# Forward block with a product-key expert layer: which token block is chosen first, and the order of its gathers and scatters

## The chip, the cores and the metric

The kernel runs on one core of one Trainium2 chip. The metric is the device time in microseconds (us) of one execution. Times of the kernel before come from three runs and from one more execution that the hardware profiler recorded.

## The reference, cut to what matters

512 tokens of width 1024 go through a mixer (a normalisation, one input projection, a gated recurrence and a short convolution, one output projection), and then through an expert layer. The change lies in the expert layer alone:

```
q  = x @ w_q                                   # 8 heads, two halves of 128
s1, s2 = q[:, :, 0] @ k1.T, q[:, :, 1] @ k2.T  # 128 scores for each half
v1, i1 = top_k(s1, 16);  v2, i2 = top_k(s2, 16)
top_s, pos = top_k(v1[:, None] + v2[None, :], 16)
idx = i1 * 128 + i2 at pos                     # 8 x 16 = 128 experts of 16384, per token
g   = softmax(top_s)
y   = sum over the 128 slots of  g * gelu(x . u_tab[idx]) * v_tab[idx]
out = layer_norm(ALPHA * x + y)
```

## The kernel before, in words

The tokens lie in four blocks of 128, numbered 0, 1, 2 (called ST, the scattered block) and 3 (called DT, the far block). The far block is worked out by gathering: for each of its 128 slots GpSimd issues an indirect DMA (`GatherPath.start`, line 1117) that brings one expert's row of u and v (8 KB) to every token's partition. VectorE multiplies it with x (`dot`, line 1136), ScalarE applies the gelu and the gate (`weigh`, lines 1143 and 1145), and VectorE adds v times that weight to the sum (`add`, line 1157). Three tiles form a ring (`RING = 3`): the gather of slot q is issued after slot q-3 was added.

The other three blocks (384 tokens) are worked out densely, for 128 blocks m of 128 experts. A product is 24 matmuls (line 952) of a block of u, split in an upper and a lower part, with x, likewise split. ScalarE makes the upper part (`upper`, line 962), GpSimd the lower part for m below 27 (`lower`, line 979) and VectorE from there (`lower_by_vector`, line 986), and ScalarE applies the gelu to the product (line 967, once for each m, so that its times are the clock of the steps). Later 18 matmuls a step (line 1746) multiply the weighted activations with v. The weights need a matrix of gates, experts by tokens, in DRAM. For blocks 0 and 1 it is made from one-hot rows: VectorE compares (line 1538), ScalarE scales (1588), TensorE multiplies (four matmuls for a group of four tokens, line 1623), ScalarE copies (1602, 1603) and stores in seven parts for each half block (line 1576, DMAs issued by ScalarE). For block 2 GpSimd scatters: 128 indirect DMAs of 4 bytes to each token's cell, added to cells that were zeroed (`scatter`, line 247); after each 16 it waits until the 16 of the head before have landed.

Stages. The query stage has 16 steps n: the projection of a half head (line 1383), the product for m = n, the scores, and the top 16 of the scores on VectorE; then three products without a projection (m = 16 to 18). The gates stage has 77 steps s = m - 19, from 0 to 76, with a product each. The expert stage has 128 steps n; in the first 64 two steps share a product and two loads of v, and from step 64 (`TAIL`) the tail loads stored activations in place of products. The last four steps are the closing ones.

Which slots are worked on when is written out by hand: `far_ops(m)` gives the number of VectorE's operations (a dot or an add) on the far block in a step, `SELECT_AT` the steps at which the eight parts of choosing a block's experts run (part 0 unpacks, 1 to 3 and 4 to 6 match, weigh and add up the two halves of the index, 7 does the softmax), `TURN_AT` and `HOT_AT` when the transposed choice and the one-hot groups come. Before, the first four heads of block 3 are chosen in the query stage (`picks`, after step 7), its gathers start at n = 12, and 10 of the 256 far operations lie in steps 13 to 16. Every engine works its list in order, so an operation that waits holds all that are behind it. The order within a step of the gates stage is, on VectorE: one-hot groups, `lower_by_vector` for the next m, the choosing, the far operations; on GpSimd: `lower` (to s = 6), gathers, scatters.

## Time and profile before

| | us |
|---|---|
| median of three runs | 1604.33 |
| lowest and highest | 1599.35, 1610.26 |
| the profiled execution, device time | 1602.93 |
| its span in the profile | 1600.9 |
| busy in it: TensorE / VectorE / ScalarE / GpSimd | 1516.2 / 1223.2 / 768.9 / 629.6 |

The span runs from the first to the last recorded instruction. Matmuls overlap, so that TensorE's busy time says little on how full it is: what a step takes is read from the distance between two gelus, and compared with the shortest such distance for the same work.

### The profile page before, as it was taken

Reading aid. Unit: us, or ns where it says so; the run is one execution under the profiler, and the core shown is the slowest. Engines: PE = TensorE matmul, PEld = TensorE weight load, DVE = VectorE, ACT = ScalarE, POOL = GpSimd, SP = SyncE. Lnnn points to the kernel's source line nnn. Section 1 sums busy time; section 2 is a strip of 40 time slices with the busy share of each in tenths; the row PEclk is TensorE's granted clock in tenths of the full one; section 3 lists DMA queues with packets and bytes.
Section 4 is the critical chain, followed back from the end, with each engine's and each line's share of the span. In section 5 each row is a group of like instructions: output and inputs, shape, how many; then the busy total and the mean of one; then the engine's idle time right before and its main releaser. Section 6 shows DMA issues by size and latency. Waiting matters only on the chain.

```text
span 1600.9 us, 21027 instructions
## 1 busy us (share of the span) xinstructions
PE 1516.2 (95%) x7484; PEld 1325.5 (83%) x7484; DVE 1223.2 (76%) x2135; ACT 768.9 (48%) x1427; POOL 629.6 (39%) x400
## 2 busy tenths in 40 slices
PE   7999999999988889999988889999999999999996
PEld 5877657799987889999988878888888888888885
DVE  7569986578997768786664488888888787888875
ACT  3559980323223467676654344444444434444432
POOL 4833352564545777788788021111111111110100
PEclk9999999999999999999999999999999999999999
DMA  7528310433535689999999999999999989999972
GB/s 270 169 94 246 92 43 0 154 109 111 191 131 173 185 229 235 231 287 258 282 257 292 346 365 348 340 342 352 344 340 346 349 316 347 353 346 356 348 249 92
DMA packets 214791, 397.00 MB, mean 248 GB/s; under 512 B 97312, under 2 KB 155040, under 8 KB 198304
## 3 DMA queue, kind: packets, MB, share of 16 engines
q1 hardware_dynamic: 110400, 242.39, 43.9%
q0 software_dynamic: 36864, 134.30, 25.6%
q10 hardware_dynamic: 67424, 18.97, 5.3%
q8 instruction: 60, 0.98, 0.2%
q14 instruction: 43, 0.35, 0.1%
HBM read 349.40 MB, written 46.20 MB: 247 GB/s over the span
## 4 chain that ended last, share of the span: by engine, by line
PE 58%; DVE 14%; POOL 13%; issue 6%; DMA 5%; ACT 2%; ACTq 1%; SPq 0%; DVEq 0%; POOLq 0%
PE bank L1746 29%; PE bank L952 16%; POOL gate_matrix L247 10%; PE bank L787 5%; PE bank L1383 2%; PE bank L842 2%; DMA gate_matrix<-gate_values,gate_cells 2%; POOL gathered L1117 2%; DMA gate_rows_then_feed<-activations 1%; DMA gathered<-in_peer_rows,expert_rows 1%; DVE xc L684 1%; PE bank L828 1%; POOL rms L487 1%; PE bank L799 1%; PE bank L1623 1%
## 5 line engine op out<-in xcount | busy, mean ns | idle before, releaser
L952 PE MATMUL bank<-xhi,ut_hi 128*128 128x384 f32 x1024 | 354.9, 347 | 29.9 <-DVE ut_lo L986 15.7
L1117 POOL DMA_INDIRECT gathered<-in_peer_rows,expert_rows x128 | 139.7, 1091 | 582.1 <-DVE gather_sum L1157 552.0
L952 PE MATMUL bank<-xhi,ut_lo 128*128 128x384 f32 x1024 | 347.8, 340 | 0.0
L952 PE MATMUL bank<-xlo,ut_hi 128*128 128x384 f32 x1024 | 347.6, 339 | 0.0
L247 POOL DMA_INDIRECT gate_matrix<-gate_values,gate_cells x128 | 240.6, 1880 | 61.3 <-issue 36.7
L1786 ACT ACTIVATE v_hi<-gate_rows_then_feed 128x1024 fp32r<-128x1024 f32 x128 | 135.7, 1061 | 224.0 <-PE bank L1746 224.0
L1746 PE MATMUL bank<-v_hi,w_hi 128*128 128x512 f32 x760 | 235.6, 391 | 6.7 <-DVE w_lo L1851 6.7
L1746 PE MATMUL bank<-v_lo,w_hi 128*128 128x512 f32 x760 | 234.9, 390 | 0.0
L1746 PE MATMUL bank<-v_hi,w_lo 128*128 128x512 f32 x760 | 234.8, 390 | 0.0
L952 PEld LDWEIGHTS bank<-xhi,ut_hi 128*128 128x128 f32 x1024 | 196.7, 192 | 36.6 <-DVE ut_lo L986 17.0
L986 DVE TENSOR_TENSOR ut_lo<-u_raw,ut_hi 128x1024 fp32r<-128x1024 f32 x101 | 123.8, 1226 | 101.1 <-ACT ut_hi L962 90.6
L952 PEld LDWEIGHTS bank<-xlo,ut_hi 128*128 128x128 f32 x1024 | 196.7, 192 | 1.7
L952 PEld LDWEIGHTS bank<-xhi,ut_lo 128*128 128x128 f32 x1024 | 195.9, 191 | 0.0
L1136 DVE SCALAR_TENSOR_TENSOR gathered<-gathered,h 128x1024 f32<-128x1024 f32 x128 | 156.0, 1220 | 42.3 <-DMA gathered<-in_peer_rows,expert_rows 34.9
L1834 DVE TENSOR_TENSOR v_lo<-gate_rows_then_feed,v_hi 128x1024 fp32r<-128x1024 f32 x128 | 156.3, 1221 | 33.1 <-ACT v_hi L1786 32.9
L967 ACT ACTIVATE gel<-bank 128x384 f32<-128x384 f32 x128 | 62.5, 489 | 231.4 <-PE bank L952 226.2
L1746 PEld LDWEIGHTS bank<-v_hi,w_hi 128*128 128x128 f32 x760 | 142.2, 188 | 36.0 <-DVE v_lo L1834 6.6
L1746 PEld LDWEIGHTS bank<-v_lo,w_hi 128*128 128x128 f32 x760 | 142.9, 188 | 30.4
L1746 PEld LDWEIGHTS bank<-v_hi,w_lo 128*128 128x128 f32 x760 | 142.9, 188 | 30.3
L1157 DVE SCALAR_TENSOR_TENSOR gather_sum<-gathered,expert_gelus,gather_sum 128x1024 f32<-128x1024 f32 x127 | 166.1, 1308 | 0.2
L962 ACT ACTIVATE ut_hi<-u_raw 128x1024 fp32r<-128x1024 f32 x128 | 135.0, 1055 | 37.8 <-issue 27.5
L979 POOL TENSOR_TENSOR ut_lo<-u_raw,ut_hi 128x1024 fp32r<-128x1024 f32 x27 | 66.2, 2454 | 85.8 <-ACT ut_hi L962 85.5
(246 smaller groups left out, 2404.8 us busy)
## 6 DMA issues: line engine op xcount, KB each, us to landing
u_raw<-in_peer_u_turned SPq DMA_DIRECT2D x128, 512.0 KB
gate_rows_then_feed<-in_peer_rows SPq DMA_DIRECT2D x128, 512.0 KB
gate_rows_then_feed<-gate_matrix SPq DMA_DIRECT2D x128, 192.0 KB
activations<-gel SPq DMA_DIRECT2D x96, 192.0 KB
gate_rows_then_feed<-activations SPq DMA_DIRECT2D x96, 192.0 KB
u_raw<-in_w_in_chunks SPq DMA_DIRECT2D x28, 512.0 KB, 4.2
gate_matrix<-gate_zeros SPq DMA_DIRECT2D x8, 1024.0 KB, 7.5
wq<-in_peer_wq_chunks SPq DMA_DIRECT2D x16, 512.0 KB, 3.9
```

The lines of the kernel that those rows point to most:

```text
L247: self.nc.gpsimd.indirect_dma_start(out=self.flat, out_offset=bass.IndirectOffsetOnAxis(ap=self.at[:, k:k + 1], axis=0), in_=self.gate[:, ...
L787: ins = mm(z_bank(n)[:, :], w[n % 2][:, k, :], x[:, k, :], start=(i == 0), stop=(i == 3 * KD - 1))
L952: ins = self.nc.tensor.matmul(self.bank[b + r % 2][:, 0:DTOK], u[r % 2][:, k, :], x[:, k, 0:DTOK], start=(i == 0), stop=(i == 3 * KD - 1))
L962: self.nc.scalar.activation(self.hi[r % 2][:, :, :], self.by_channel(r), ACT.Copy).then_inc(self.hi_ready, 1)
L979: self.nc.gpsimd.tensor_tensor(out=self.lo[r % 2][:, :, :], in0=self.by_channel(r), in1=self.hi[r % 2][:, :, :].bitcast(F32), op=ALU.subtr ...
L986: self.nc.vector.tensor_tensor(out=self.lo[r % 2][:, :, :], in0=self.by_channel(r), in1=self.hi[r % 2][:, :, :].bitcast(F32), op=ALU.subtr ...
L1117: self.nc.gpsimd.indirect_dma_start(out=self.tile[q % RING][:, :], out_offset=None, in_=self.table, in_offset=bass.IndirectOffsetOnAxis(ap ...
L1136: self.nc.vector.scalar_tensor_tensor(out=half, in0=half, scalar=1.0, in1=self.x, op0=ALU.mult, op1=ALU.mult, accum_out=self.act[:, q:q + ...
L1157: ins = V.scalar_tensor_tensor(out=self.sum[:, :], in0=half, scalar=weight, in1=self.sum[:, :], op0=ALU.mult, op1=ALU.add)
L1746: ins = mm(bank[2 + 2 * tb + half][:, :], w[r][:, tb * P:(tb + 1) * P], v[r][:, half * HALF_D:(half + 1) * HALF_D], start=begins, stop=ends)
L1786: S.activation(v_hi[r][:, :], v_raw[r][:, :], ACT.Copy).then_inc(v_hi_ready, 1)
L1834: V.tensor_tensor(out=v_lo[r][:, :], in0=v_raw[r][:, :], in1=v_hi[r][:, :].bitcast(F32), op=ALU.subtract).then_inc(v_lo_ready, 1)
```

## The change

- The first four heads chosen in the query stage are block 2's, not block 3's, and their cells are listed there (`list_cells`). Scatters start at step 13 of the query stage: two a step, one a step for m = 16 to 25, then two a step until s = 62 (before: from s = 7 to 66).
- Block 3's whole choice is made at s = 2 to 5; its gathers start at s = 6 (before at n = 12) and its operations at s = 8. At the end of the gates stage 59 far operations have been done (before 75).
- Block 0 is chosen at s = 7 to 14 (before 4 to 8) and block 1 at 28 to 35 (before 20 to 27). The 64 one-hot groups lie in s = 16 to 64 (before 10 to 63).
- The order of far operations becomes dot 0, add 0, dot 1, add 1 (before dot 0, dot 1, add 0, dot 2, add 1). A step of the expert stage begins with the add of the slot whose dot ended the step before.
- In the tail the far operations come at 9 in 7 steps (before 1 a step), and end at n = 119 (before 117).

```diff
...
 BY_POOL = 7
-SELECT_AT = {ST: (0, 0, 1, 1, 2, 2, 3, 3), 0: (4, 4, 5, 5, 6, 6, 7, 8), 1: tuple(range(20, 28)),
-             DT: tuple(range(32, 40))}
-TURN_AT = {9: 0, 29: 1}
-HOT_AT, HOT_STEPS = 10, 54
-SCATTER_AT, SCATTER_STEPS = 7, 60
+SELECT_AT = {ST: (0, 0, 0, 0, 1, 1, 1, 1), DT: (2, 2, 3, 3, 4, 4, 5, 5), 0: tuple(range(7, 15)),
+             1: tuple(range(28, 36))}
+TURN_AT = {15: 0, 36: 1}
+HOT_AT, HOT_STEPS = 16, 49
+FIRST_GATHER = 6
...
     s = m - BY_QUERIES
+    if s < FIRST_GATHER + 2 or 28 <= s < 36:
+        return 0
+    return 1 - s % 2 if 9 < s < 15 else 1
+def scatters(m):
     if m < QC - 3:
         return 0
-    if s < 0:
-        return 2 if m < QC else 4 if m == QC else 0
-    if s < HOT_AT or 20 <= s < 28:
-        return 0
-    return 2 if s in (11, 13, 15, 17, 19, 29) else 1
+    return 2 if m < QC else 1 if m < BY_QUERIES + BY_POOL else 2
+SCATTERED_BY = [min(SLOTS, sum(scatters(e) for e in range(m))) for m in range(MADE + 1)]
 FAR_BY = [sum(far_ops(e) for e in range(m)) for m in range(MADE + 1)]
...
             key = rb("key", [P, TB, QH, 2, TOPK], U32)
+            cells.hold(rb)
             with ExitStack() as st:
-                asked = queries(nc, a, sem, st, bank, h, ident, iota, pB, xhi, xlo, acts, far, act_dram, top, pos, key,
-                                mixed)
+                asked = queries(nc, a, sem, st, bank, h, ident, iota, pB, xhi, xlo, acts, act_dram, top, pos, key, mixed,
+                                cells)
             shared = rb("gate_rows_then_feed", [P, ExpertFeed.GATE_ROWS, P])
             feed = ExpertFeed(a, sem, shared.rearrange("p i t -> p (i t)"), act_dram, gates_dram)
-            cells.hold(rb)
             made = gates(nc, sem, bank, ident, iota, acts, far, act_dram, top, pos, key, gates_dram, shared, feed, cells,
...
+    def list_cells(self, eng, link, sel, q, n):
+        V, at, size = self.nc.vector, slice(q * TOPK, (q + n) * TOPK), n * TOPK
+        link(V.scalar_tensor_tensor(out=self.row[:, at], in0=sel[:, 0, 0:size], scalar=float(KEYS),
+                                    in1=sel[:, 1, 0:size], op0=ALU.mult, op1=ALU.add))
+        if q == 0:
+            eng.wait_ge(self.token_ready, 1)
+        link(V.tensor_scalar(out=self.at[:, at], in0=self.row[:, at], scalar1=float(DTOK),
+                             scalar2=self.token[:, 0:1], op0=ALU.mult, op1=ALU.add))
+        V.sem_inc(self.listed, 1)
     def scatter(self, eng, k):
...
             eng.wait_ge(self.zeroed, 16 * self.ZEROED)
-            eng.wait_ge(self.listed, 1)
+        if k in (0, EARLY_HEADS * TOPK):
+            eng.wait_ge(self.listed, 1 + k // (EARLY_HEADS * TOPK))
         if k % TOPK == 0 and q > 0:
...
-    def list_rows(self, link, far, q, n):
-        link(self.nc.vector.scalar_tensor_tensor(
-            out=far.rows[:, q * TOPK:(q + n) * TOPK], in0=self.sel[:, 0, 0:n * TOPK], scalar=float(KEYS),
-            in1=self.sel[:, 1, 0:n * TOPK], op0=ALU.mult, op1=ALU.add))
+    def list_rows(self, link, far):
+        link(self.nc.vector.scalar_tensor_tensor(out=far.rows[:, :], in0=self.sel[:, 0, :], scalar=float(KEYS),
+                                                 in1=self.sel[:, 1, :], op0=ALU.mult, op1=ALU.add))
         self.nc.vector.sem_inc(far.listed, 1)
...
-        return min(SLOTS, 1 + ops // 2) if ops else 0
+        return (ops + 1) // 2
...
-        return SLOTS if ops == 2 * SLOTS else max(0, (ops - 1) // 2)
+        return ops // 2
...
-        if q in (0, EARLY_HEADS * TOPK):
-            eng.wait_ge(self.listed, 1 + q // (EARLY_HEADS * TOPK))
+        if q == 0:
+            eng.wait_ge(self.listed, 1)
         after(eng, self.added, q - RING + 1)
...
-        if i == 2 * SLOTS - 1:
-            self.add(eng, SLOTS - 1)
-        elif i == 0 or i % 2 == 1:
-            self.dot(eng, (i + 1) // 2)
+        if i % 2:
+            self.add(eng, i // 2)
         else:
-            self.add(eng, i // 2 - 1)
+            self.dot(eng, i // 2)
...
-def queries(nc, a, sem, st, bank, h, ident, iota, pB, xhi, xlo, acts, far, act_dram, top, pos, key, mixed):
+def queries(nc, a, sem, st, bank, h, ident, iota, pB, xhi, xlo, acts, act_dram, top, pos, key, mixed, cells):
...
     PICK_AT = 2 * EARLY_HEADS - 1
-    started_by = lambda n: 0 if n < QC - 4 else far.started(FAR_BY[n])
-    weighed_by = lambda n: far.products(FAR_BY[n])
-    assert PICK_AT + 5 <= QC - 4
     ln = sb("ln1", [P, 2, D])
...
                 picks.exponent(eng, 1, EARLY_HEADS)
-            for q in range(weighed_by(n - 1) if n else 0, weighed_by(n)):
-                far.weigh(eng, q)
             acts.gelu_to_store(eng, n, n, n // GELS)
...
             acts.upper(eng, m + 1, m + 1, (m + 1) // UB + 1)
-            if m == QC:
-                for q in range(weighed_by(QC - 1), weighed_by(QC)):
-                    far.weigh(eng, q)
             acts.gelu_to_store(eng, m, m, m // GELS)
...
                 link(G.tensor_tensor(out=blk, in0=blk, in1=ln[:, 1, :], op=ALU.add))
-            for q in range(started_by(n - 1), started_by(n)):
-                far.start(eng, q)
+            for k in range(SCATTERED_BY[n], SCATTERED_BY[n + 1]):
+                cells.scatter(eng, k)
         for m in range(QC - 1, BY_QUERIES + 1):
             acts.lower(eng, m, m)
-            if m == QC:
-                for q in range(started_by(QC - 1), started_by(QC)):
-                    far.start(eng, q)
+            if QC <= m < BY_QUERIES:
+                for k in range(SCATTERED_BY[m], SCATTERED_BY[m + 1]):
+                    cells.scatter(eng, k)
...
             q, side = n // 2, n % 2
-            for e in range(FAR_BY[n], FAR_BY[n + 1]):
-                far.use(eng, e)
             eng.wait_ge(s_done, n + 1)
...
             if n == PICK_AT:
-                picks.places(link, DT, 0, EARLY_HEADS)
+                picks.places(link, ST, 0, EARLY_HEADS)
                 picks.match(link, 0, EARLY_HEADS)
...
             elif n == PICK_AT + 2:
-                link(picks.softmax(eng, link, 1, EARLY_HEADS, far.gate[:, 0:EARLY_HEADS * TOPK]))
-                picks.list_rows(link, far, 0, EARLY_HEADS)
-        for e in range(FAR_BY[QC], FAR_BY[QC + 1]):
-            far.use(eng, e)
+                link(picks.softmax(eng, link, 1, EARLY_HEADS, cells.gate[:, 0:EARLY_HEADS * TOPK]))
+                cells.list_cells(eng, link, picks.sel, 0, EARLY_HEADS)
...
-    scattered_by = lambda s: min(SLOTS, max(s - SCATTER_AT, 0) * SLOTS // SCATTER_STEPS)
     first_load = MADE - 8
-    assert last_step(3) + PARTS < first_load + feed.SLOT - BY_QUERIES and scattered_by(first_load - BY_QUERIES) == SLOTS
-    weighed_by = lambda s: far.products(FAR_BY[BY_QUERIES + s if s > 3 else QC])
+    assert last_step(3) + PARTS < first_load + feed.SLOT - BY_QUERIES and SCATTERED_BY[first_load] == SLOTS
+    weighed_by = lambda s: far.products(FAR_BY[BY_QUERIES + s])
+    started_by = lambda s: far.started(FAR_BY[BY_QUERIES + s]) if s >= FIRST_GATHER else 0
...
         nth = {tb: i for i, tb in enumerate(SELECT_AT)}
-        heads_of = lambda tb: (EARLY_HEADS, QH - EARLY_HEADS) if tb == DT else (0, QH)
+        heads_of = lambda tb: (EARLY_HEADS, QH - EARLY_HEADS) if tb == ST else (0, QH)
...
                     if part == 3:
-                        after(eng, selT_done, {ST: 0, 0: 0, 1: 1, DT: 2}[tb])
+                        after(eng, selT_done, int(tb == 1))
                     picks.add_up(link, part // 4, n)
                 elif tb == DT:
-                    link(picks.softmax(eng, link, nth[DT] + 1, n, far.gate[:, q * TOPK:(q + n) * TOPK]))
-                    picks.list_rows(link, far, q, n)
-                elif tb < ST:
+                    link(picks.softmax(eng, link, nth[DT] + 1, n, far.gate[:, :]))
+                    picks.list_rows(link, far)
+                elif tb == ST:
+                    link(picks.softmax(eng, link, nth[tb] + 1, n, cells.gate[:, q * TOPK:(q + n) * TOPK]))
+                    cells.list_cells(eng, link, sel, q, n)
+                else:
                     picks.softmax(eng, link, nth[tb] + 1, QH, sel[:, 2, :]).then_inc(sel_ready, 1)
-                else:
-                    link(picks.softmax(eng, link, nth[tb] + 1, QH, cells.gate[:, :]))
-                    link(V.scalar_tensor_tensor(out=cells.row[:, :], in0=sel[:, 0, :], scalar=float(KEYS),
-                                                in1=sel[:, 1, :], op0=ALU.mult, op1=ALU.add))
-                    eng.wait_ge(cells.token_ready, 1)
-                    link(V.tensor_scalar(out=cells.at[:, :], in0=cells.row[:, :], scalar1=float(DTOK),
-                                         scalar2=cells.token[:, 0:1], op0=ALU.mult, op1=ALU.add))
-                    V.sem_inc(cells.listed, 1)
...
                     acts.lower(eng, m + 1, m + 1)
-                for q in range(far.started(FAR_BY[m - 1 if s else QC]), far.started(FAR_BY[m])):
+                for q in range(started_by(s - 1), started_by(s)):
                     far.start(eng, q)
-                for k in range(scattered_by(s), scattered_by(s + 1)):
+                for k in range(SCATTERED_BY[m], SCATTERED_BY[m + 1]):
                     cells.scatter(eng, k)
...
-    far_by = lambda n: min(2 * SLOTS, FAR_FROM + 2 * min(n, TAIL) + max(n - TAIL, 0))
+    assert FAR_FROM % 2 == 1
+    far_plan = [FAR_FROM + 2 * n for n in range(TAIL + 1)]
+    for n in range(TAIL, STEPS):
+        far_plan.append(min(2 * SLOTS, far_plan[-1] + 1 + int(
+            far_plan[-1] % 2 == 1 and far_plan[-1] - far_plan[TAIL] < (n - TAIL) * 9 // 7)))
+    far_by = lambda n: far_plan[n]
     FAR_DONE = min(n for n in range(STEPS) if far_by(n) >= 2 * SLOTS)
...
```

## Rows read from the trace of the kernel before

**Rows 1.** Windows: busy us (instructions) of PE, PEld, DVE, ACT, POOL; clock; DMA share; GB/s.

```profile
700.00:800.00 100.00, 96.19 (x598) 94.83 (x597) 69.39 (x71) 68.08 (x180) 77.99 (x45) 0.98 1.02 277
...
860.00:890.00 30.00, 22.49 (x115) 20.97 (x113) 10.94 (x12) 6.63 (x12) 15.65 (x10) 0.94 1.15 355
...
1000.00:1100.00 100.00, 100.00 (x486) 88.28 (x485) 82.06 (x105) 44.02 (x84) 16.92 (x17) 1.00 0.93 342
...
1330.00:1520.00 190.00, 189.28 (x835) 156.09 (x834) 155.29 (x209) 78.99 (x141) 22.23 (x23) 1.00 0.99 352
```

**Rows 2.** The chain that ended last: start, us, what.

```profile
486.75 8.39 DMA gathered<-in_peer_rows,expert_rows
...
848.93 1.78 PE bank L1623 x16
...
850.71 8.35 PE bank L952 x48
...
869.95 3.89 ACTq L1576
...
875.79 6.16 issue
...
1443.88 122.92 PE bank L1746 x540
```

**Rows 3.** Timeline of ScalarE, the gelu of m = 13, 14, 15, 22, 27, 81, 95.

```profile
441.20 0.49 ACT L967 ACTIVATE gel<-bank 128x384 f32<-128x384 f32 x1 [1.75 <-PE bank L952]
...
451.76 0.49 ACT L967 ACTIVATE gel<-bank 128x384 f32<-128x384 f32 x1 [1.86 <-PE bank L952]
...
469.02 0.49 ACT L967 ACTIVATE gel<-bank 128x384 f32<-128x384 f32 x1 [8.99 <-PE bank L952]
...
509.82 0.49 ACT L967 ACTIVATE gel<-bank 128x384 f32<-128x384 f32 x1 [8.60 <-PE bank L952]
...
537.84 0.49 ACT L967 ACTIVATE gel<-bank 128x384 f32<-128x384 f32 x1 [8.32 <-PE bank L952]
...
843.96 0.49 ACT L967 ACTIVATE gel<-bank 128x384 f32<-128x384 f32 x1 [1.04 <-PE bank L952]
...
920.71 0.49 ACT L967 ACTIVATE gel<-bank 128x384 f32<-128x384 f32 x1 [0.33 <-PE bank L952]
```

**Rows 4.** Timeline of GpSimd at the end of the query stage.

```profile
458.36 1.69 POOL L1117 DMA_INDIRECT gathered<-in_peer_rows,expert_rows  x1 [14.10 <-DVE gather_sum L1155]
```

**Rows 5.** Timeline of VectorE, last far operations of m = 16, then choosing; one ScalarE row.

```profile
484.29 3.40 DVE L1157 SCALAR_TENSOR_TENSOR gather_sum<-gathered,expert_gelus,gather_sum 128x1024 f32<-128x1024 f32 x1
...
495.16 1.23 DVE L1136 SCALAR_TENSOR_TENSOR gathered<-gathered,h 128x1024 f32<-128x1024 f32 x1 [7.47 <-DMA gathered<-in_peer_rows,expert_rows]
...
496.52 0.29 DVE L1015 TENSOR_TENSOR ex_late<-top 128x128 f32<-128x128 f32 x1
...
514.68 0.29 DVE L1015 TENSOR_TENSOR ex_late<-top 128x128 f32<-128x128 f32 x1
...
497.17 1.28 ACT L967 ACT_TABLE_LOAD   x1
```

**Rows 6.** GpSimd's groups from 523.5 to 877 us: count, busy and mean ns, idle before.

```profile
L247 POOL DMA_INDIRECT gate_matrix<-gate_values,gate_cells x128 | 240.6, 1880 | 61.3 <-issue 36.7 <-DMA gate_matrix<-gate_values,gate_cells 24.6
...
L1117 POOL DMA_INDIRECT gathered<-in_peer_rows,expert_rows x28 | 37.4, 1336 | 14.3 <-issue 8.2 <-DVE gather_sum L1157 6.1
```

**Rows 7.** Page, part 5: GpSimd's lower parts in the whole span.

```profile
L979 POOL TENSOR_TENSOR ut_lo<-u_raw,ut_hi 128x1024 fp32r<-128x1024 f32 x27 | 66.2, 2454 | 85.8 <-ACT ut_hi L962 85.5
```

**Rows 8.** DMA queue of GpSimd, 700 to 800 us: packets, MB, share of 16 engines.

```profile
q0 software_dynamic: 6305, 8.41, 34.9%
```

**Rows 9.** DMA queues from 1330 to 1520 us.

```profile
q1 hardware_dynamic: 19851, 42.19, 64.0%
...
q0 software_dynamic: 3379, 24.62, 34.8%
```

**Rows 10.** VectorE's group that waits for loads, 1330 to 1520 us.

```profile
L1846 DVE TENSOR_TENSOR w<-gate_rows_then_feed 128x384 f32<-128x384 f32 x46 | 25.6, 557 | 15.8 <-DMA gate_rows_then_feed<-activations 14.1 <-issue 1.5
```

## The prediction

> **What bounds the kernel now.** I read the windows first [rows 1]. From 1000 to 1100 us TensorE is never idle at a full clock; from 1330 to 1520 us it is full too, and so are the DMA engines (share 0.99 at 352 GB/s). From 700 to 800 us GpSimd shows 78 busy, VectorE 69, and TensorE's own row looks full but isn't: the distance between gelus tells. The floor of a step comes from the chain [rows 2]: 48 matmuls of a product in 8.35 us, so 4.17 a step; two one-hot groups (16 matmul instructions) in 1.78, so 0.89 a group; 540 matmuls of the tail in 122.92, so 30 steps of 4.10. A query step takes 10.56 (441.20 to 451.76, [rows 3]). Against these floors the gelus of [rows 3] give three stretches:
>
> m = 14 to 27 (s = 8), 451.76 to 537.84: 86.1 us; the floor is 10.56 + 12 x 4.17 = 60.6; lost 25.5.
> s = 8 to 62, 537.84 to 843.96: 306.1 us; 54 x 4.17 + 61 groups x 0.89 = 279.5; lost 26.6.
> s = 62 to 76, to 920.71: 76.8 us; 14 x 4.17 + 3 x 0.89 = 61.1; lost 15.7.
>
> The first loss has the far block behind it. GpSimd stands 14.10 us for the first add before it issues gather 3 [rows 4], the lower part for m = 15 is queued behind, and its product comes late (17.26 us from gelu to gelu in place of 10.56, 6.7 lost). Then VectorE ends an add at 487.7, waits 7.47 us for a gather and only then begins to choose block 2, at 496.5 [rows 5]; ScalarE, whose exponential needs that, holds the gelu and the upper parts behind it. Seven products take 40.8 us to 509.82 in place of 29.2 (11.6 lost), and the five to 537.84 28.0 in place of 20.8 (7.2 lost), because choosing two blocks at 18.2 us each (496.52 to 514.68, [rows 5]) keeps VectorE from its first lower parts.
>
> The second loss is GpSimd's. Between 523.5 and 877 us it does 128 scatters at 1.88 us and 28 gathers at 1.34, with about 0.3 before each, and 24.6 us of waits for the landing of 16 scatters, seven times; only 6.1 us are a wait for VectorE [rows 6]. So it is late all the way, a gather behind late scatters is late, and VectorE waits for it with the next lower part behind. The third is the last half block's store beside everything else: DMA share 1.15 from 860 to 890 [rows 1], and ScalarE held in its own DMA issues (3.89, then 6.16 us, [rows 2]).
>
> **The change, part by part.** *Query stage.* The ten far operations, their weighing and the waits for them leave; choosing four heads costs the same for block 2 as for block 3. The 25.5 us lost go as far as their causes: 6.7 and 11.6 wholly, 7.2 too, since VectorE begins to choose at about 474 (the far operations that end at 487.7 take some 7 us, so 480.7, less the 6.7) and needs 9 us for half a block and 18.2 for block 3, so it is done near 505, before its first lower part is due (about 513). What is late next is GpSimd. For m = 16 to 25 a scatter stands between two lower parts; 2.45 for a lower part [rows 7] + 1.88 for a scatter [rows 6] + two gaps of 0.2 = 4.75 against 4.17, ten times: +5.8. Bounds: 0, if the scatter falls in the wait for ScalarE, and 10 x 2.2 = 22, if all of each scatter lies outside that wait. I stay near the low end, since the cadence of GpSimd's own work gives it. In steps 13 to 15 two scatters (4.4 us) fit in the 14.10 us that [rows 4] shows idle: nothing, and +4 for each step if that cover were gone. Two exponentials fall in steps where GpSimd still makes the lower part; each brings ScalarE a table load of 1.28 before the gelu [rows 5], about 1.4 each: +2.8. The first gathers are issued at s = 6 behind the wait for block 3's list, land 8.39 us later [rows 2], and are wanted at s = 8, some 9 us on: +2 (0 to 6; queued behind the wait are only scatters). The two more list operations of 0.3 us on VectorE are hidden in its lead. Sum: -25.5 + 10.6 = -14.9.
>
> *s = 8 to 62.* GpSimd has from s = 7 to 62, 56 steps, 112 scatters x 2.18 = 244, 7 landings x 3.5 = 24.6 and 22 gathers x 1.64 = 36: 305 us. TensorE needs 56 x 4.17 + 61 x 0.89 = 288. GpSimd would end 17 late, and 5 more from its late start behind the three first gathers: 22. Whether that holds TensorE depends on the lead of a gather. Before, gather q is issued after add q-3, and dot q comes three operations later; now five. At one operation a step of 5.3 us that is 4 whole steps from GpSimd's turn to the dot instead of 2: 21 us plus some 3 us of place in the step, less 9.7 for issue and landing [rows 2, 6], so GpSimd may be 14 to 16 us late at no cost, where before it might be 4 to 6. The lateness by sums: 5 at s = 7, 15 at s = 16 (steps of only 4.17, with 18 scatters, but only each second step wants a gather), 18 at s = 28, 14 at s = 36 (no gathers in between), 19 at s = 62. Over the allowance: about 4. To that I add 3 for ScalarE, where a step with two groups meets a store, and 3 for VectorE, which in s = 7 to 14 has 18.2 + 8 lower parts and 5 far operations of about 1.23 each [rows 5] = 34 us in 33 of the floor, and for slower landings on full DMA queues. Lost 10 in place of 26.6: -16.6, less nothing for the groups (60 by then, 61 before; the one comes back after). The bounds are 0 lost (-26.6) and GpSimd's pace as now (0). The waits on the transposed choice hide: block 1's third part at s = 31 wants the transpose of s = 15.
>
> *s = 62 to 76.* Four groups instead of three, +0.9; no scatters beside the store. From 700 to 800 us GpSimd's queue has 34.9 us of 16 engines; 8.41 MB are 8 gathers at 2.81 (below), which leaves 12.4 for the other 37 of the window's 45 instructions [rows 1], 0.34 each [rows 8]; two a step over five steps: -3. The store's parts move one step later, to s = 64 to 70, and SyncE's waits for them at s = 69 and 73 are then 3 steps behind: 12 us, nothing, or up to +5 if they land later. Sum -2 (-8 to +5).
>
> *Expert stage to step 64.* Two far operations a step as before; TensorE full, DMA share 0.93: 0.
>
> *Tail.* At its start 96 gathers are issued where it was 104, so 8 more of 1.05 MB fall into it. From 1330 to 1520 us there are 46 steps [rows 10], of 4.13. Queue q1 takes 0.640 of 190 us, 2.64 a step; q0 takes 0.348 with 23.5 gathers (24.62 MB), 2.81 each [rows 9]. Before: 2.64 + 2.81/2 = 4.05 of 4.13. After, with 9/14 of a gather a step: 2.64 + 1.81 = 4.45. TensorE's 4.10 no longer hides it. Over the 49 steps until the last gather: 49 x (4.45 - 4.13) = +15.7, less some 2.7 for loads that stand ready in four buffers at the start: **+13**. Bounds: 0, if the engines can go above their 352 GB/s, and 8 x 2.81 = 22. VectorE waited 14.1 us in all for the activations' loads there [rows 10]; it was busy 155 of 190 us [rows 1], 3.4 a step, and 2/7 of an operation more makes 3.8: it hides. The far block's end moves from step 117 to 119, still before the closing steps: 0.
>
> The sum on the profiled execution: 1602.9 - 14.9 - 16.6 - 2 + 13 = 1582.4. The median stands 1.4 above that execution: **1584**.
>
> What the Trainium skill says on the tail: "DMA: Bandwidth & Descriptors", under "Where 436 GB/s comes from", puts the HBM limit of a core near 358 GB/s for loads like these, and under "Measured (HBM→SBUF, 128 partitions, SWDGE, issued from GpSimd)" it has 425 GB/s for a core whose neighbour is idle, as here. By the first an estimate of the tail step is 1.59 MB / 358 = 4.45 us, by the second 3.75. The trace has 352 at share 0.99.
>
> **The rivals.** *A, the tail is free.* The queues reach 355 GB/s at a share of 1.15 [rows 1], so the share isn't a hard stop. Against: over 190 us it stays at 0.99, and TensorE already sits at its floor only just. 1584 - 13 = **1571**. The page's second figure says this too.
>
> *B, GpSimd still paces the middle.* The lead helps only if lateness is bounded; 305 us of work against 288 is nearly the ratio of now. From 700 to 800 us the queues stand at 1.02 [rows 1], and a faster pace asks more of them, so landings lengthen, and each microsecond goes to GpSimd. Then the 16.6 don't come: 1584 + 17 = **1601**. This is also the case in which the new order of dot and add does nothing.
>
> *C, slower.* The last half block's store costs 15.7 us because products run at 4.17 us and DMA is overfull. The three other half blocks (parts now at s = 28 to 34, 40 to 46, 52 to 58) are stored almost free today since GpSimd slows the steps. If at the faster pace ScalarE is held in its issues there as well (6.16 us an issue, [rows 2]), each costs as much: 1584 + 3 x 14 = **1626**. It decides from three of the three; two give 1612. Against: the stretch of 306.1 us holds three such stores already, and GpSimd's sum explains all that it lost.
>
> **How the numbers follow.** A change of less than 1% can't be told from none here: 1588.3 and 1620.4 are the marks. Forecast (1576 to 1594) 0.45; A 0.16; B 0.30; C 0.09. The range, to hold 8 in 10, reaches from A's less 2 to B's plus 4: 1569 to 1605. Faster by over 1%: A and two thirds of the forecast and a little, 0.49; slower 0.08; within 1% 0.43.
>
> **What the profile after would show.** Gelu of m = 15 10.6 us after that of m = 14; the first half block of choosing near 474; the gelu of s = 8 at about 523, of s = 62 at about 812, of s = 76 at about 887. No wait of VectorE for a gather before s = 20, GpSimd still busy without a break from s = 7 to 62. In the tail 4.45 us a step to step 113, waits of VectorE for the activations' loads of several times the 14.1 us, and TensorE idle there. The prediction is wrong if the tail step stays at 4.13 (A), if s = 8 to 62 takes over 300 us (B), or if ScalarE's store issues appear in the chain before s = 62 (C).

## The result, and the profile after

Seven runs of the changed kernel have a median of 1594.61 us (1583.99 to 1596.48), seven of the kernel before on the same chip 1608.24: a ratio of 0.9913, interval 0.9887 to 0.9938. The change gains 0.9%. The forecast was 1584, the stated range 1569 to 1605; rival B had 1601. The profiled execution took 1594.78 with a span of 1592.8, 8.1 under that of before. The page of the kernel after, its first lines:

```profile
span 1592.8 us, 21032 instructions
...
PE 1509.7 (95%) x7484; PEld 1315.5 (83%) x7484; DVE 1227.1 (77%) x2136; ACT 770.8 (48%) x1427; POOL 686.2 (43%) x400
```

As before, the gelus are the clock of the steps. ScalarE's timeline after, m = 14, 15, 22, 27, 81 and 95 (the answer to [rows 3]; the line is now 984):

```profile
451.84 0.49 ACT L984 ACTIVATE gel<-bank 128x384 f32<-128x384 f32 x1 [2.70 <-PE bank L969]
462.40 0.49 ACT L984 ACTIVATE gel<-bank 128x384 f32<-128x384 f32 x1 [2.70 <-PE bank L969]
...
496.47 0.49 ACT L984 ACTIVATE gel<-bank 128x384 f32<-128x384 f32 x1
...
522.08 0.49 ACT L984 ACTIVATE gel<-bank 128x384 f32<-128x384 f32 x1
...
824.13 0.49 ACT L984 ACTIVATE gel<-bank 128x384 f32<-128x384 f32 x1 [1.47 <-PE bank L969]
...
905.21 0.47 ACT L984 ACTIVATE gel<-bank 128x384 f32<-128x384 f32 x1
```

The stretches, each the difference of two such starts, the first of them the start itself (the tail from VectorE's first weights operation of step 64 to that of step 127):

| stretch | before | after | got | forecast |
|---|---|---|---|---|
| s = 8, its gelu | 537.84 | 522.08 | -15.8 | -14.9 |
| s = 8 to 62 | 306.1 | 302.0 | -4.1 | -16.6 |
| s = 62 to 76 | 76.8 | 81.1 | +4.3 | -2 |
| s = 76 to the last gelu (m = 127) | 395.8 | 395.6 | -0.2 | 0 |
| tail, steps 64 to 127 | 254.2 | 261.7 | +7.5 | +13 |

They sum to -8.3, the spans to -8.1. The query stage did what it should, the middle nearly nothing, and the stretch with the last half block's store and the tail gave back 11.8. The 3.7 us between the last gelu and step 64 are in no row; they are the same before and after (3.7 and 3.8). GpSimd's groups after, 512 to 850 us, answer to [rows 6]:

```profile
L264 POOL DMA_INDIRECT gate_matrix<-gate_values,gate_cells x113 | 218.2, 1931 | 68.9 <-DMA gate_matrix<-gate_values,gate_cells 36.6 <-issue 32.3
...
L1133 POOL DMA_INDIRECT gathered<-in_peer_rows,expert_rows x27 | 39.4, 1459 | 9.2 <-issue 7.9 <-DVEq L1085 1.3
```

The seven waits for 16 landings are 36.6 us here and were 24.6. GpSimd is still what the middle hangs on: of the chain that ended last, followed from 522 to 824 us, 58.7% are scatters, 15.8% their landings and 8.5% the issue of gathers. GpSimd's timeline after, where block 3's gathers begin, shows the first of them:

```profile
513.34 2.00 POOL L1133 DMA_INDIRECT gathered<-in_peer_rows,expert_rows  x1 [1.28 <-DVEq L1085]
515.64 0.97 POOL L1133 DMA_INDIRECT gathered<-in_peer_rows,expert_rows  x1 [0.30 <-issue]
516.92 0.94 POOL L1133 DMA_INDIRECT gathered<-in_peer_rows,expert_rows  x1 [0.30 <-issue]
518.16 1.60 POOL L264 DMA_INDIRECT gate_matrix<-gate_values,gate_cells  x1 [0.30 <-issue]
529.13 1.55 POOL L264 DMA_INDIRECT gate_matrix<-gate_values,gate_cells  x1 [9.37 <-DMA gate_matrix<-gate_values,gate_cells]
```

Three gathers of 1 MB go out, then the 16th scatter; the 17th must wait until that one has landed, and stands 9.37 us. The seven waits are 9.37, 1.73, 3.73, 5.20, 7.57, 3.65 and 5.38 us; ahead of the 7.57 a gather had been issued at 693.45 and the head's last scatter at 696.88. What VectorE waited for in 522 to 824 us (us in total, times, longest):

```profile
DVE gathered L1150 <- DMA gathered<-in_peer_rows,expert_rows: 25.5, 8, 5.9
```

It was 19.1 us in 8 waits before: five operations of lead did not take these waits away.

The chain from 844 to 880 us shows the store of the last half block, as [rows 2] did:

```profile
849.04 12.58 ACTq L1572
...
864.09 10.28 PE bank L969 x48
```

ScalarE is held 12.58 us in one DMA issue, with the next upper part and gelu behind it, and TensorE stands still. The longest issue of this store before was 8.09 us, but more of them were long: the seven issues sum to 26.2 us before and to 19.0 after. The length of the holds alone doesn't tell why the stretch grew. The windows tell what the queues did meanwhile, and what the tail (44 of its steps) did:

```profile
850.00:860.00 10.00, 3.47 (x21) 3.15 (x19) 0.17 (x1) 0.00 (x0) 0.94 (x1) 0.88 1.02 414
...
1320.00:1510.00 190.00, 185.32 (x806) 149.73 (x805) 162.26 (x220) 80.54 (x145) 37.48 (x29) 1.00 1.00 373
```

In the tail TensorE is idle for 4.7 us of 190 (it was 0.7, [rows 1]) and 373 GB/s pass at a share of 1.00, where it was 352 at 0.99. The queues there, and VectorE's group that waits for the loads (the answers to [rows 9, 10]):

```profile
q1 hardware_dynamic: 19324, 41.11, 59.0%
q0 software_dynamic: 4083, 29.65, 40.5%
```

```profile
L1847 DVE TENSOR_TENSOR w<-gate_rows_then_feed 128x384 f32<-128x384 f32 x44 | 24.5, 556 | 21.9 <-DMA gate_rows_then_feed<-activations 21.9
```

In 190 us the queue q0 moved 28.3 gathers instead of 23.5, and the waits for loads are 21.9 instead of 14.1 us.

### The profile page after: what moved, and what is told of

Its sections match the earlier page's. It is cut to its first block, busy times and chain, and to the rows that moved or that the text cites. A ratio compares the mean times of both kernels' runs of the same rounds, so it can differ in the third digit from the quotient of the medians.

```text
span 1592.8 us, 21032 instructions
## 1 busy us (share of the span) xinstructions
PE 1509.7 (95%) x7484; PEld 1315.5 (83%) x7484; DVE 1227.1 (77%) x2136; ACT 770.8 (48%) x1427; POOL 686.2 (43%) x400
## 4 chain that ended last, share of the span: by engine, by line
PE 50%; POOL 14%; DVE 13%; DMA 13%; issue 5%; ACT 3%; ACTq 1%; SPq 0%; DVEq 0%; POOLq 0%
PE bank L1747 20%; PE bank L969 15%; POOL gate_matrix L264 11%; DMA gate_rows_then_feed<-activations 8%; PE bank L804 5%; PE bank L1388 5%; DMA gate_matrix<-gate_values,gate_cells 3%; PE bank L859 2%; POOL gathered L1133 2%; DMA gate_matrix<-stage 1%; DVE xc L701 1%; DVE gather_sum L1171 1%; DVE w L1847 1%; PE bank L1376 1%; POOL rms L504 1%
## 5 line engine op out<-in xcount | busy, mean ns | idle before, releaser
L1133 POOL DMA_INDIRECT gathered<-in_peer_rows,expert_rows x128 | 191.6, 1497 | 524.6 <-DVE gather_sum L1171 515.4
L264 POOL DMA_INDIRECT gate_matrix<-gate_values,gate_cells x128 | 245.5, 1918 | 72.9 <-DMA gate_matrix<-gate_values,gate_cells 36.6
L1171 DVE SCALAR_TENSOR_TENSOR gather_sum<-gathered,expert_gelus,gather_sum 128x1024 f32<-128x1024 f32 x127 | 162.3, 1278 | 0.0
L1791 ACT ACTIVATE w_hi<-w 128x384 fp32r<-128x384 f32 x128 | 67.0, 523 | 74.1 <-DVE w L1847 74.1
```

The lines of the kernel that those rows point to most:

```text
L264: self.nc.gpsimd.indirect_dma_start(out=self.flat, out_offset=bass.IndirectOffsetOnAxis(ap=self.at[:, k:k + 1], axis=0), in_=self.gate[:, ...
L1133: self.nc.gpsimd.indirect_dma_start(out=self.tile[q % RING][:, :], out_offset=None, in_=self.table, in_offset=bass.IndirectOffsetOnAxis(ap ...
L1171: ins = V.scalar_tensor_tensor(out=self.sum[:, :], in0=half, scalar=weight, in1=self.sum[:, :], op0=ALU.mult, op1=ALU.add)
```

## The experiments

Ratios are to the kernel before on the same chip, with their interval; stretches are of the profiled execution. All edits are on the kernel after, but for the fourth. Three dots stand for lines left out.

**1. The old order of dot and add.**

```diff
-        return (ops + 1) // 2
+        return min(SLOTS, 1 + ops // 2) if ops else 0
...
-        return ops // 2
+        return SLOTS if ops == 2 * SLOTS else max(0, (ops - 1) // 2)
```

with `use` as before.

> The changed kernel with the old order of dots and adds (dot 0, dot 1, add 0, dot 2, ...), all else as changed. Theory 1, my prediction's: the new order gives a gather two operations more of lead, and that is worth time where GpSimd is late and where the tail's DMA queues are full; then s = 8 to 62 takes 10 us or more longer than the changed kernel's 302, or the tail from step 64 to 127 takes some us longer than its 262, and the whole is 1604 to 1612. Theory 2: the lead is worth nothing, because GpSimd's own sum of work is the bound; then every stretch is within 3 us of the changed kernel's and the whole is 1592 to 1597.

Measured: 1591.18 us, 0.9905 (0.988 to 0.9929). s = 8 to 62 took 296.2, 5.8 less than with the new order. Gelus of s = 8 and 62:

```profile
521.95 0.49 ACT L984 ACTIVATE gel<-bank 128x384 f32<-128x384 f32 x1
...
818.17 0.49 ACT L984 ACTIVATE gel<-bank 128x384 f32<-128x384 f32 x1 [1.04 <-PE bank L969]
```

It is the second theory's side, though not within the 3 us that it allowed. Two later runs have this kernel's plan up to s = 62 and give 301.9 and 306.5 (experiments 6 and 7), and two have the changed kernel's and give 299.6 and 295.1 (experiments 3 and 5). So a middle of the same plan spreads over some 7 to 10 us from run to run, and no difference between the orders stands clear of that. The longer lead, the ground of my forecast for the middle, was worth nothing that can be seen in this kernel. The other stretches: s = 62 to 76 took 76.2 (after: 81.1) and the tail 264.7 (261.7). The landing waits sum to 23.0 us here, though the scatters are the same.

**2. Half the scatters.** Every second scatter is left out, so half of block 2's gates are missing.

```diff
+        if k % 2:
+            return
         self.nc.gpsimd.indirect_dma_start(
```

> The changed kernel with every second scatter left out (block 2 gets half its gates), the landing waits kept on those that are left. Theory 1: GpSimd's own work is the bound from s = 8 to 62; with half the scatters it has about 190 us for 56 steps, and the stretch falls from 302 to near its floor of 279, at most 285. Theory 2: the bound is the DMA engines' load, or ScalarE with two groups beside a store; the scatters are a small part of the DMA share, so the stretch stays above 293. The last stretch, s = 62 to 76, should stay near 81 in either.

Measured: 1571.35 us, 0.9782 (0.9738 to 0.9826). s = 8 to 62 took 288.9, 13.1 less than after, and s = 62 to 76 76.6:

```profile
521.02 0.49 ACT L986 ACTIVATE gel<-bank 128x384 f32<-128x384 f32 x1
...
809.88 0.49 ACT L986 ACTIVATE gel<-bank 128x384 f32<-128x384 f32 x1 [1.47 <-PE bank L971]
```

That lies between the two theories' bounds (285 and 293). GpSimd still paced the middle of the changed kernel. About 289 is what is left with half of the scatters; the other 10 over the floor of 279 were not won by relieving GpSimd. The landing waits still sum to 32.6 us in this run, nearly as in the changed kernel: long waits alone do no harm when GpSimd has work to spare.

**3. Eight slots fewer.** The last eight slots of block 3 are left out (`FAR_SLOTS` is 120), and the tail goes at one operation a step.

```diff
-            far_plan[-1] % 2 == 1 and far_plan[-1] - far_plan[TAIL] < (n - TAIL) * 9 // 7)))
+        far_plan.append(min(2 * FAR_SLOTS, far_plan[-1] + 1))
```

> The changed kernel with the last 8 slots of block 3 left out, so that the tail has one far operation a step as the kernel before had it. Theory 1: the tail pays for 8 more gathers on full DMA queues; the tail from step 64 to 127 falls from 261.7 us to 254, what the kernel before took, and the time by 7 to 8. Theory 2: the tail's loss comes from the two operations in one step on VectorE, or from something of the new order, not from the bytes; since this kernel also has no double steps in the tail, that part can't be told from theory 1 by the time alone but by the DMA share: under theory 1 it is below 1.00 and the waits for the activations' loads fall from the changed kernel's; if the new order were to blame they stay. If the tail stays at 262, the eight gathers cost nothing.

Measured: 1586.23 us, 0.9867 (0.9819 to 0.9915). The tail took 256.0, 5.7 less than after. Its window, and the waits:

```profile
1320.00:1510.00 190.00, 187.21 (x825) 154.37 (x824) 155.46 (x210) 78.74 (x141) 22.11 (x22) 1.00 0.96 349
```

```profile
L1847 DVE TENSOR_TENSOR w<-gate_rows_then_feed 128x384 f32<-128x384 f32 x47 | 26.1, 555 | 12.8 <-DMA gate_rows_then_feed<-activations 12.7
```

The share fell below 1.00 and the waits from 21.9 to 12.7, as the first theory had it. The eight gathers at 9 operations in 7 steps cost 5.7 us here, where the forecast had 13; the later tails say more on this.

**4. The kernel before, without its far operations in the query stage.** Its ten operations there move to the tail, at 9 in 7 steps; all else is the kernel before.

```diff
-    if s < 0:
-        return 2 if m < QC else 4 if m == QC else 0
```

> The kernel before with its ten far operations of the query stage taken out and given to the tail (9 in 7 steps there), nothing else changed: block 3's first heads are still chosen first, the scatters start at s = 7. Theory 1: the query stage's far operations alone cost what the change won there; the gelu of m = 15 comes at 462.4 in place of 469.0, that of s = 3 near 494 in place of 509.8, and that of s = 8 near 523 or a little above, since choosing blocks 2 and 0 in s = 0 to 8 still crowds VectorE. Then the middle stays as before (306) and the tail pays 3 to 5 us for 5 more gathers: 1590 to 1597. Theory 2: the gain at s = 8 comes from where the choosing lies, not from the far operations; then s = 8 stays above 531 and the time is 1603 to 1610.

Measured: 1598.63 us, 0.995 (0.993 to 0.997). The gelu of m = 15, then of s = 8:

```profile
462.03 0.49 ACT L965 ACTIVATE gel<-bank 128x384 f32<-128x384 f32 x1 [2.70 <-PE bank L950]
...
523.07 0.49 ACT L965 ACTIVATE gel<-bank 128x384 f32<-128x384 f32 x1 [9.34 <-PE bank L950]
```

14.8 us earlier than in [rows 3], of the 15.8 that the whole change has there. The gain up to s = 8 is the far block's leaving; that block 2 is chosen first and scattered early brings only the last 1.0. That is as the first theory had it. The middle took 305.0, as before. The tail did not: 264.8 instead of 254.2, so 10.6 us for five more gathers, where 3 to 5 were expected, and the total came out above the 1590 to 1597 of that theory.

**5. No far operations in s = 63 to 70.** The last four slots of block 3 are left out, so the tail's load stays near that of after.

```diff
-    if s < FIRST_GATHER + 2 or 28 <= s < 36:
+    if s < FIRST_GATHER + 2 or 28 <= s < 36 or 63 <= s < 71:
```

> The changed kernel with no far operation in s = 63 to 70 (four gathers fewer there) and the last 4 slots of block 3 left out, so that the tail has the changed kernel's number of gathers. Theory 1: the loss from s = 62 to 76 (81 us against a floor of 62) is ScalarE held in the issue of the last half block's stores by DMA queues that the gathers help to fill; without four gathers (11 us of the 16 engines) the stretch falls to 70 to 75 and the time to 1583 to 1588. Theory 2: the stores' own 256-byte packets hold ScalarE; the stretch stays within 3 us of 81.

Measured: 1581.23 us, 0.9869 (0.9828 to 0.9911). The gelus of s = 62 and 76, and the longest hold of ScalarE in an issue of the store, from the chain:

```profile
815.71 0.49 ACT L985 ACTIVATE gel<-bank 128x384 f32<-128x384 f32 x1 [1.47 <-PE bank L970]
...
884.89 0.47 ACT L985 ACTIVATE gel<-bank 128x384 f32<-128x384 f32 x1
```

```profile
840.61 2.80 ACTq L1573
```

69.2 us from s = 62 to 76 instead of 81.1, and 2.80 in an issue instead of 12.58. The gathers beside the store cost 11.9 of the 19.1 over the floor of 61.9 (four groups now). The middle took 295.1 with an unchanged plan, 6.9 less than after.

**6 and 7. Nine far operations in four live steps** (a live step is one of the expert stage's first 64; old order of dot and add), without and with the pause of experiment 5. The tail has one operation a step in 6, and 9 in 7 in 7. Nothing is left out.

```diff
-    far_plan = [FAR_FROM + 2 * n for n in range(TAIL + 1)]
+    far_plan = [FAR_FROM + 2 * n + n // 4 for n in range(TAIL + 1)]
```

> The changed kernel with the old order of dots and adds and with nine far operations in four steps (before 2 a step) in the first 64 steps of the expert stage; the tail then has one a step, as the kernel before. Theory 1: eight gathers cost the tail 6 to 8 us, and from step 0 to 64, where TensorE is full and the DMA share is 0.91 to 0.93, they are free; that stretch stays at 396 us, the tail falls to about 255, and the time is 1583 to 1587. Theory 2: the DMA share there would be 0.97, and loads come late to TensorE in that stretch too; it grows by 4 us or more and nothing is won.

> As e6, but also no far operation in s = 63 to 70; the four gathers that this puts off are paid in the tail, which has 9 operations in 7 steps again until they are done. Nothing is left out. Theory 1: from s = 62 to 76 it wins 5 to 10 us as e5 does, and the tail pays 3 to 4 of them back: 1579 to 1585. Theory 2 (stores hold ScalarE by themselves): no gain there, the tail's cost alone: 1587 to 1591.

Measured: 1615.98 us, 1.0064 (1.0025 to 1.0102), and 1618.74, 1.0076 (1.0053 to 1.01). From s = 76 to the last gelu they took 425.9 and 429.7 instead of 395.6, where the first theory had no loss at all. The group of VectorE that pays for it, 930 to 1290 us, and the window (experiment 6):

```profile
L1152 DVE SCALAR_TENSOR_TENSOR gathered<-gathered,h 128x1024 f32<-128x1024 f32 x60 | 73.3, 1222 | 61.6 <-DMA gathered<-in_peer_rows,expert_rows 61.6
```

```profile
930.00:1290.00 360.00, 338.28 (x1611) 291.82 (x1610) 288.78 (x369) 141.58 (x282) 67.99 (x61) 1.00 0.92 337
```

The DMA engines are not full (0.92) and VectorE is busy 289 of 360, yet it waits 61.6 us for gathers. From this I take it (it is not shown) that the time from the issue of a gather (7.3 us to its landing, in the median) to its dot binds, with three tiles and the old order. Whether the new order, with its longer lead, bears nine in four was not tried. The pause did its part again: s = 62 to 76 took 72.9 without and 65.5 with it. The tails took 253.2 and 261.7.

**8. No scatters in m = 16 to 25.** Ten scatters go from between the lower parts to s = 62 to 66.

```diff
-    return 2 if m < QC else 1 if m < BY_QUERIES + BY_POOL else 2
+    return 2 if m < QC else 0 if m < BY_QUERIES + BY_POOL else 2
```

> The changed kernel without its ten scatters in m = 16 to 25, where each stands between two of GpSimd's lower parts; they follow at the end, to s = 67. Theory 1, my prediction's: those ten cost 5.8 us by s = 7, since GpSimd's cadence of 4.75 us stands in place of TensorE's 4.17; without them the gelu of s = 8 comes at 516 to 518 in place of 522, and the ten scatters (22 us of GpSimd) come back later, so that s = 8 to 62 is longer by 0 to 6. Theory 2: the loss there is VectorE's choosing and ScalarE's two table loads; the gelu of s = 8 stays at 521 to 523.

Measured: 1578.59 us, 0.9837 (0.9812 to 0.9862): better than both kernels, and complete. Gelus of s = 8 and 62, and GpSimd's scatters, 512 to 852 us:

```profile
519.25 0.49 ACT L984 ACTIVATE gel<-bank 128x384 f32<-128x384 f32 x1
...
806.75 0.49 ACT L984 ACTIVATE gel<-bank 128x384 f32<-128x384 f32 x1 [1.49 <-PE bank L969]
```

```profile
L264 POOL DMA_INDIRECT gate_matrix<-gate_values,gate_cells x122 | 238.6, 1956 | 55.8 <-issue 35.4 <-DMA gate_matrix<-gate_values,gate_cells 20.5
```

s = 8 came 2.8 us earlier, where the first theory had 4 to 6. The middle took 287.5, 14.5 less, with the same plan for GpSimd from s = 7 to 62; it had been expected to be longer by 0 to 6, so neither theory had this. The landing waits fell by 16.1, from 36.6 to 20.5. GpSimd also has less behind it when s = 7 begins; this run does not part the two.

**9. No scatters in m = 16 to 25, four more in the idle steps 12 to 15.**

```diff
-    if m < QC - 3:
-        return 0
-    return 2 if m < QC else 1 if m < BY_QUERIES + BY_POOL else 2
+    if m < QC:
+        return {12: 3, 13: 2, 14: 3, 15: 2}.get(m, 0)
+    return 0 if m < BY_QUERIES + BY_POOL else 2
```

> The changed kernel with ten scatters in steps 12 to 15 of the query stage (3, 2, 3, 2), where GpSimd stands idle, none in m = 16 to 25, then two a step to s = 65. Theory 1: what held the changed kernel from s = 8 is that its 17th scatter, at s = 7, waits for the landing of the 16th, which was issued right behind the first three gathers, and that GpSimd starts there 9 us late; with ten early scatters the 17th comes at s = 10. The gelu of s = 8 comes at 519, s = 8 to 62 takes 285 to 291, the scatters end some 8 us earlier than without the four more early ones, and the time is 1574 to 1580. Theory 2: the kernel without the ten scatters was only lucky in how its waits fell; then s = 8 to 62 is anywhere from 287 to 302.

Measured: 1579.7 us, 0.9829 (0.9783 to 0.9874), with the middle at 289.8. s = 8 came at 521.5, not at 519: from the gelu of m = 11 to that of m = 12 it took 14.3 us instead of 10.6. GpSimd stands 7.66 us for VectorE's list before the first scatter of step 12, and the lower part is behind it, so these scatters were not free. The landing waits sum to 11.5 us, less than in any run above, and the middle is no faster for it. GpSimd's timeline where the longest of after stood (lines between them left out):

```profile
530.74 2.06 POOL L1133 DMA_INDIRECT gathered<-in_peer_rows,expert_rows  x1 [0.30 <-issue]
...
533.83 2.87 POOL L264 DMA_INDIRECT gate_matrix<-gate_values,gate_cells  x1 [1.04 <-DMA gate_matrix<-gate_values,gate_cells]
```

**10. Experiment 9 with the pause at s = 63 to 70, and the tail at 10 in 7** (complete).

```diff
-            far_plan[-1] % 2 == 1 and far_plan[-1] - far_plan[TAIL] < (n - TAIL) * 9 // 7)))
+            far_plan[-1] % 2 == 1 and far_plan[-1] - far_plan[TAIL] < (n - TAIL) * 10 // 7)))
```

> As e9, with no far operation in s = 63 to 70, and 10 operations in 7 steps in the tail, so that nothing is left out. Theory: s = 62 to 76 falls from 80 to 69 or 70 as in e5, and four more gathers in the tail cost 3 us (the eight of the change cost 5.7): 1566 to 1574. Rival: at 10 in 7 the tail's step comes to 4.6 us and takes back all that was won: 1576 to 1582.

Measured: 1584.73 us, 0.9855 (0.9806 to 0.9903), no better than experiment 9. Both expectations missed, the rival by 3 us. s = 62 to 76 fell from 77.3 to 66.8, and none of the store's seven issues took more than 0.37 us, now that no gather is issued beside them:

```profile
844.56 0.37 ACTq L1572 DMA_DIRECT2D gate_matrix<-stage  x1
```

But the tail rose from 264.1 to 282.5, where 3 us had been expected. The windows of 10 and of 9:

```profile
1290.00:1510.00 220.00, 205.23 (x864) 164.85 (x863) 178.95 (x243) 87.41 (x161) 49.92 (x34) 0.97 0.97 361
```

```profile
1290.00:1510.00 220.00, 212.49 (x924) 171.74 (x923) 185.04 (x251) 92.99 (x167) 41.09 (x32) 1.00 0.99 367
```

The tail, with four gathers more and at 10 in 7, took away what the pause gave. The profiled execution is the slowest of four (1593.12, the fastest 1580.2), so 18.4 is more than the median shows, and with the DMA share at 0.97 why this tail is so slow stays open.

**11. No gathers before s = 62**, and 23 slots of block 3 left out to hold the tail's load.

```diff
-    if s < FIRST_GATHER + 2 or 28 <= s < 36:
+    if s < 64:
```

> The changed kernel without any gather from s = 6 to 61; 23 of block 3's slots are left out, so that the expert stage is as in the changed kernel. Theory 1: a wait for 16 scatters to land is long because gathers of 1 MB stand before them in GpSimd's own queue; without gathers the seven waits fall from 36.6 us to 15 or less, none above 3, and s = 8 to 62 takes 280 to 285. Theory 2: the other queues make the landing slow; the waits stay above 25 us in sum, though TensorE may still be faster, since nothing waits for a gather.

Measured: 1578.18 us, 0.9817 (0.9776 to 0.9859). The middle took 288.1, not 280 to 285: the same plateau that experiments 2 and 8 reached from other sides. The landing waits sum to 19.1 us, the longest 4.77, with no gather issued ahead of any of them; that lies between the two theories, which had 15 or less with none above 3, and over 25. Up to the first of these waits the kernel differs from the changed one in the three gathers alone, and there it waits 2.74 us instead of 9.37:

```profile
516.50 1.55 POOL L265 DMA_INDIRECT gate_matrix<-gate_values,gate_cells  x1 [2.74 <-DMA gate_matrix<-gate_values,gate_cells]
```

So the gathers made that wait longer by 6.6 us, and the rest of the waits is not theirs.

**12. Experiment 8 with the old order of dot and add.**

> As e8 (no scatters in m = 16 to 25), but with the old order of dots and adds. It tests the lead of two operations with GpSimd less late. Theory 1: the lead is worth something once GpSimd's lateness is within it; s = 8 to 62 takes 292 or more where e8 took 287.5. Theory 2: the order is worth nothing in the gates stage; 285 to 290. In the tail (65 gathers' worth of full DMA queues) both should show 262 to 265.

Measured: 1591.74 us, 0.9906 (0.9874 to 0.9939). Gelus of s = 8 and 62, and GpSimd's scatters, 512 to 855 us:

```profile
517.69 0.49 ACT L984 ACTIVATE gel<-bank 128x384 f32<-128x384 f32 x1
...
824.37 0.49 ACT L984 ACTIVATE gel<-bank 128x384 f32<-128x384 f32 x1 [1.04 <-PE bank L969]
```

```profile
L264 POOL DMA_INDIRECT gate_matrix<-gate_values,gate_cells x122 | 230.0, 1886 | 65.0 <-issue 35.1 <-DMA gate_matrix<-gate_values,gate_cells 29.9
```

306.7 us for the middle against 287.5 with the new order, which is more than the 7 to 10 us by which such middles spread, and 13 us in the medians, with intervals of the ratio that do not touch. So the new order does work, once the ten scatters ahead of s = 7 are gone. In the kernel as changed it was not to be seen (experiment 1).

## Why the prediction was right or wrong

**Up to s = 8: right.** -14.9 forecast, -15.8 got. Choosing began at 475.6 (forecast near 474), m = 15 came 10.56 us after m = 14, and experiment 4 shows that the far block's leaving is 14.8 of it. The added cost of a scatter between two lower parts was put at 5.8; taking the ten away gave 2.8, so the sign and the end of the bounds near which I stayed were right, and the size was twice too large. VectorE's first wait for a gather came at 582.4, after s = 20 (578.0), as forecast.

**s = 8 to 62: the step that failed**, by 12.5 us, and it is rival B's case. I wrote "lost 10 in place of 26.6"; 23.4 stayed lost. Two of its terms fell. First GpSimd's sum: 305 us and 5 for its start were forecast, and from its first gather at 513.3 to the end of its last scatter at 844.4 it took 331. 12.0 of the 21 between are landing waits, taken over as seven times 3.5 from the kernel before; 6.4 are scatters (113 at 1.931 and 0.29 of issue, where I had 112 at 2.18); the rest are gathers (1.459 in place of 1.336). A wait for a landing is no property of the scatter alone: with three gathers just ahead it was 9.37 us, without them 2.74 (experiment 11). Second the allowance of 14 to 16 us that the lead should give: experiment 1 shows nothing of it in this kernel. Experiments 8 and 12 together show that it exists, 19.2 us in the middle, once the ten scatters ahead of s = 7 are gone. With a spread of 7 to 10 us between middles of the same plan, the 4.1 won here can't be told from nothing.

Side by side, the sum of the landing waits and the middle. New order: 11.3 us and 292.9 (10), 11.5 and 289.8 (9), 19.1 and 288.1 (11), 20.5 and 287.5 (8), 31.9 and 295.1 (5), 33.7 and 299.6 (3), 36.6 and 302.0 (after), and 32.6 and 288.9 with half the scatters (2). Old order: 20.3 and 301.9 (6), 20.3 and 306.5 (7), 20.9 and 305.0 (4), 23.0 and 296.2 (1), 24.6 and 306.1 (before), 29.9 and 306.7 (12). With the new order and all scatters the middle is slower where the waits are above some 30 us, and below some 20 they no longer matter. With the old order there is no such relation. That the waits are the cause, and not GpSimd's work altogether, is not shown: experiment 2 has the long waits and a short middle. What is shown is that relieving GpSimd in four ways (2, 8, 9 with 10, 11) brings the middle to 287.5 to 292.9 with the new order. In experiment 8 the chain of this stretch still runs through GpSimd (63.4% scatters), in 9 and 11 through TensorE's products (63.4 and 73.8%), so at about 288 the two are near balance; what holds the last 9 us over the floor of 279 stays open.

That a gather ahead of a head's last scatter makes the wait long is tested by experiment 11 for the first wait alone. For the 7.57, with a gather 3.4 us ahead, and for the 1.04 of experiment 9, with one issued just behind that scatter, it is read from the timelines.

**s = 62 to 76:** forecast -2, got +4.3; I had named up to +5 for slower landings on other grounds. What was late next was ScalarE, held 12.58 us in a single issue. Experiment 5 gives 11.9 us for four gathers beside the store. But the plan asks for those gathers before as well as after, so they are no cost of the change by themselves. The traces show what differs: between the gelus of s = 62 and 76 GpSimd issued 9 gathers after and 7 before, since it was late and had issued only 23 by s = 62 where the plan has 25. Over all runs, the gathers issued in this stretch and its length: 3 and 65.5 or 66.8 (7, 10), 5 and 69.2 (5), 6 and 75.5 (11), 7 and 72.9 to 77.1 (6, 1, 2, before, 12), 8 and 76.8 or 77.3 (4, 9), 9 and 79.8 to 82.8 (8, after, 3). So the term I had left out is that gathers late in the middle slip into this stretch, at some 2.5 us each by these rows. Where none lies beside the store, its issues take 0.37 us. Rival C, the same at the other three half blocks, did not come: the middle reaches 287.5 with all three stores in it, and no store issue is in the changed kernel's chain from s = 8 to 62.

**Expert stage to step 64:** 0 forecast, -0.2 got.

**Tail: mechanism right, size off.** +13 forecast, +7.5 got. The step became 4.30 us to step 113 (210.7 / 49), where 4.45 was forecast and 4.10 is TensorE's floor. I took 352 GB/s for the ceiling because the share stood at 0.99; 373 passed. A packet's time wasn't fixed (queue q1 took 2.64 us of the 16 engines a step before, and 0.590 x 190 / 44 = 2.55 after), so a share near 1 did not mean full. Rival A (free) is wrong too: experiment 3 shows 5.7 us for the eight gathers.

How the cost splits is less clear. The tails with one operation a step took 253.2 (6), 254.2 (before) and 256.0 (3); those at 9 in 7 with the new order 258.4 to 266.6 (2, 5, after, 8, 9, 11), all with 69 operations, so one value is good to some 4 us; and experiments 4 and 7, at 9 in 7 with only five and four gathers more than at one a step, took 264.8 and 261.7, as much as the ones with eight more and the same old order (264.7 and 261.0, experiments 1 and 12). So the cost seems to go with the pace of 9 in 7 rather than with the number of gathers, and 5.7/8 is no price of a gather.

The limit near 358 GB/s in the Trainium skill ("DMA: Bandwidth & Descriptors", "Where 436 GB/s comes from"), which the prediction set beside its own 4.45, does not agree with the 373 over 190 us. The 425 that the same page has under "Measured (HBM→SBUF, 128 partitions, SWDGE, issued from GpSimd)", for a core whose neighbour is idle, was not reached here.

The total, 1594.61 against 1584, is the middle's 12.5 and the store's 6.3 on one side, and the tail's 5.5 and the query stage's 0.9 on the other: 12.4 in the profiled execution (1594.78 against 1582.4). The medians differ by 10.6, since I had added 1.4 from the profiled execution to the median and here the median lies 0.2 below it. That the total stayed in the range is in part luck: the change came out in the band of less than 1%, to which I gave 0.43, with rival B's middle and a tail that cost 5.5 less than forecast.

## What to carry to other kernels

A large gather issued just ahead of small scatters can lengthen the wait for their landing (9.37 us against 2.74 here): keep it away from the last scatter ahead of such a wait, and don't carry the mean wait of the old schedule into a new one. An engine that is late all the way must be relieved before a longer lead further down can show its worth; try both together before the lead is called useless. Work that such an engine puts off ends in the next stage, so price what it lies beside there: two late gathers came to lie beside the store, eight more lay in the tail by plan, and of the query stage's 15.8 us 11.8 were lost again. And measure how far two runs of the same plan differ in a stretch before a difference in it is given a cause: here it was 7 to 10 us of 300.

## What had not been expected of the hardware

- One DMA issue on ScalarE held the engine 12.58 us while the 16 DMA engines moved 414 GB/s for 10 us at a share of 1.02; with four gathers fewer beside it the longest hold was 2.80, and with none (experiment 10) each issue took 0.37.
- 352 GB/s at a share of 0.99 was no ceiling: the same tail moved 373 GB/s over 190 us when asked for more.
- The issue of a scatter took 1.93 us in the mean and 1.54 at the least; the wait for a head's 16 landings was between 1.73 and 9.37 us in the changed kernel, and 2.74 in place of 9.37 without three gathers just ahead.
- With nine far operations in four steps, three tiles in the ring and the old order, VectorE waited 61.6 of 360 us for gathers at a DMA share of 0.92.
